# One added wait in the seven-product stage, and the first attention's transposes in three groups

## What is computed

```python
def forgetting_attention(q, k, v, logf):
    for s0 in range(0, s_len, Q_BLOCK):             # Q_BLOCK = 128
        logits = q[s0:s1] @ k[:s1].T * scale + c[s0:s1] - c[:s1]
        logits = where(kpos <= qpos, logits, -inf)
        p = softmax(logits)
        outs.append(p @ v[:s1])

def swiglu(h, w_gate_up, w_down):                   # 1024 -> 2 x 2816 -> 1024
    g, u = split(h @ w_gate_up)
    return (silu(g) * u) @ w_down
```

## Time and profile before

| | us |
|---|---|
| median of 3 timed runs | 1335.58 (1335.21 to 1336.49) |
| profiled execution, its own time | 1338.37 |
| its span, first to last instruction | 1336.6 |
| PE busy | 1313.5 (98%) |
| DVE busy | 774.5 (58%) |
| ACT busy | 614.4 (46%) |
| POOL busy | 358.3 (27%) |

### The profile page before, as it was taken

One profiled execution on the slowest core, in us unless ns is written; L12 is line 12 of the kernel. 1 busy time (PEld: TensorE's weight loads), 2 busy tenths in 40 slices (PEclk: granted clock), 3 DMA queues, 4 the chain that ended last, 5 costly groups with the idle time before them and its releaser, 6 DMA issues.

```text
span 1336.6 us, 18442 instructions
## 1 busy us (share of the span) xinstructions
PE 1313.5 (98%) x7206; PEld 1093.9 (82%) x7206; DVE 774.5 (58%) x1544; ACT 614.4 (46%) x1315; POOL 358.3 (27%) x246
## 2 busy tenths in 40 slices
PE   7999999999999999999999999999999999999999
PEld 6777887888889999998887877877878787777777
DVE  4416574333479887877234656566666666666643
ACT  4325565222435444445224446454656555556430
POOL 4013310000046556540002404142322424144210
PEclk8999999999999999999999999999999999999999
DMA  7303232332442343233235222222222222323311
GB/s 241 102 16 90 78 95 64 95 95 95 158 157 87 104 127 116 75 127 111 79 108 207 95 65 71 94 74 93 79 72 72 72 72 71 103 71 125 140 59 63
DMA packets 110103, 130.87 MB, mean 98 GB/s; under 512 B 7488, under 2 KB 87360, under 8 KB 110016
## 3 DMA queue, kind: packets, MB, share of 16 engines
q1 hardware_dynamic: 104400, 112.39, 26.3%
q10 hardware_dynamic: 5616, 17.30, 3.5%
HBM read 120.24 MB, written 9.44 MB: 97 GB/s over the span
## 4 chain that ended last, share of the span: by engine, by line
PE 81%; DVE 10%; ACT 4%; POOL 2%; issue 2%; DMA 0%; ACTq 0%; DVEq 0%
PE ps L812 13%; PE ps L814 12%; PE ps L813 12%; PE ps L817 6%; PE ps L819 6%; PE ps L818 6%; PE ps L1019 5%; PE ps L1022 5%; PE ps L1021 5%; DVE wlo L1443 3%; PE ps L1077 2%; POOL rq L1814 2%; ACT px L1394 2%; PE ps L1087 1%; ACT whi L1142 1%
## 5 line engine op out<-in xcount | busy, mean ns | idle before, releaser
L1443 DVE TENSOR_TENSOR wlo<-raw,whi 128x512 fp32r<-128x512 f32 (+1 forms) x262 | 220.0, 860 | 185.0 <-ACT whi L1142 184.3
L1142 ACT ACTIVATE whi<-raw 128x512 fp32r<-128x512 f32 (+2 forms) x338 | 210.8, 651 | 126.9 <-PE ps L814 81.8
L812 PE MATMUL ps<-whi,hth 128*128 128x512 f32 x592 | 247.7, 418 | 2.6 <-DVE wlo L1443 2.6
L814 PE MATMUL ps<-wlo,hth 128*128 128x512 f32 x592 | 233.2, 394 | 0.0
L813 PE MATMUL ps<-whi,htl 128*128 128x512 f32 x592 | 232.6, 393 | 0.0
L1844 POOL TENSOR_TENSOR wlo<-raw,whi 128x512 fp32r<-128x512 f32 (+1 forms) x76 | 91.8, 1223 | 435.4 <-ACT whi L1142 435.4
L812 PEld LDWEIGHTS ps<-whi,hth 128*128 128x128 f32 x592 | 112.1, 189 | 34.2 <-issue 9.2
L814 PEld LDWEIGHTS ps<-wlo,hth 128*128 128x128 f32 x592 | 112.0, 189 | 25.7
L813 PEld LDWEIGHTS ps<-whi,htl 128*128 128x128 f32 x592 | 112.4, 190 | 18.4
L1394 ACT ACTIVATE px<-px,nm 128x128 f32<-128x128 f32 (+3 forms) x128 | 70.7, 554 | 112.6 <-DVE nm L1758 105.0
L817 PE MATMUL ps<-hth,whi 128*128 128x512 f32 (+1 forms) x288 | 112.5, 391 | 0.0
(11 more groups left out here) (339 smaller groups left out, 2880.7 us busy)
## 6 DMA issues: line engine op xcount, KB each, us to landing
raw<-in_l_w_in SPq DMA_DIRECT2D x64, 512.0 KB, 4.7
raw<-in_w_gate_up SPq DMA_DIRECT2D x44, 512.0 KB, 4.9
raw<-in_w_in SPq DMA_DIRECT2D x14, 1024.0 KB, 5.4
raw<-in_w_down SPq DMA_DIRECT2D x10, 1024.0 KB, 5.0
raw<-in_l_w_out SPq DMA_DIRECT2D x8, 1024.0 KB, 5.2
raw<-in_w_in SPq DMA_DIRECT2D x24, 256.0 KB, 3.7
raw<-in_w_branch SPq DMA_DIRECT2D x8, 512.0 KB, 4.1
raw<-in_w_out SPq DMA_DIRECT2D x4, 1024.0 KB, 5.1
```

The source lines that it names most:

```text
L812: e.matmul(o, ah, wh[:, cs], start=a, stop=False)
L814: m = e.matmul(o, ah, wl[:, cs], start=False, stop=z)
L1142: return e.activation(out, in_, ACT.Copy, **how)
L1443: return e.tensor_tensor(out, src, hi_part.bitcast(F32), ALU.subtract)
```

## The change

The first part adds one wait to POOL's queue: the sum number 4 (T3 of block 2) starts only when `comb_d` says that U3 of block 1 is done. The second part regroups the transposes of the first attention. The ten tiles of a head go into three groups in place of four: key block 0 (4 tiles), key block 1 (3 tiles), and key blocks 2 and 3 together (3 tiles). The layout in `pth` and `ptl` stays as it was, since key block 3's columns lie right behind key block 2's. The semaphores count three a head, and `pv` waits for the third group before its key blocks 2 and 3. One bank a head fewer is dealt.

```diff
@@ attn1
             for h in (2 * j, 2 * j + 1):
-                for kb in range(TB):
-                    put("tu", h, kb, self.bank())
-                    if kb % 2:
-                        yield
+                put("tu", h, 0, self.bank())
+                put("tu", h, 1, self.bank())
+                yield
+                put("tu", h, 2, self.bank())
+                yield
                 yield
                 put("pv", h, self.bank())
@@ build
+        TILES = [[(0, qb) for qb in range(TB)], [(1, qb) for qb in range(1, TB)], [(2, 2), (2, 3), (3, 3)]]
@@ PE
                 elif kind == "tu":
-                    h, kb, b = a
+                    h, i, b = a
                     claim(b)
-                    for qb in range(kb, TB):
-                        pe.wait_ge(pn_a, AT1(h, TB - 1))
-                        m = e.transpose(ps[b][:, P * (qb - kb):P * (qb - kb) + P],
+                    pe.wait_ge(pn_a, AT1(h, TB - 1))
+                    for c, (kb, qb) in enumerate(TILES[i]):
+                        m = e.transpose(ps[b][:, P * c:P * c + P],
                                         sx[h % 2][:, QSEG[qb] + P * kb:QSEG[qb] + P * kb + P], ident[:])
                     m.then_inc(tu_pe, 1)
-                    free[b] = [(pt_lo, 4 * h + kb + 1)]
+                    free[b] = [(pt_lo, 3 * h + i + 1)]
@@ PE, pv
-                        pe.wait_ge(pt_lo, 4 * h + kb + 1)
+                        pe.wait_ge(pt_lo, 3 * h + min(kb, 2) + 1)
@@ ACT
-                    h, kb, b = a
-                    n = S - P * kb
-                    act.wait_ge(tu_pe, 4 * h + kb + 1)
+                    h, i, b = a
+                    n = P * len(TILES[i])
+                    act.wait_ge(tu_pe, 3 * h + i + 1)
...
-                    copy(pth[:, KSEG[kb]:KSEG[kb] + n], ps[b][:, 0:n]).then_inc(pt_hi, 1)
+                    copy(pth[:, KSEG[i]:KSEG[i] + n], ps[b][:, 0:n]).then_inc(pt_hi, 1)
@@ DVE
-                    dve.wait_ge(pt_hi, 4 * h + kb + 1)
+                    dve.wait_ge(pt_hi, 3 * h + i + 1)
                     lower(ptl[:, cs], ps[b][:, 0:n], pth[:, cs]).then_inc(pt_lo, 1)
@@ POOL, wt
                     else:
                         pool.wait_ge(mm, MIX_DONE)
+                    if q == 4:
+                        pool.wait_ge(comb_d, COMB(1, U3))
                     pool.wait_ge(t_p, q)
```

More of the change, by code:

```diff
@@ L1257, in _ @@
                     if j == 0:
-                        act.wait_ge(tu_pe, 4 * H1 - (4 if i == 0 else 0))
+                        act.wait_ge(tu_pe, 3 * H1 - (3 if i == 0 else 0))
                     else:
@@ L1584, in _ @@
                             if h >= 2:
-                                dve.wait_ge(tu_pe, 4 * h - 4)
+                                dve.wait_ge(tu_pe, 3 * h - 3)
                             e.tensor_tensor_reduce(
@@ L1597, in _ @@
                 elif kind == "tu":
-                    h, kb, b = a
-                    n = S - P * kb
-                    cs = slice(KSEG[kb], KSEG[kb] + n)
-                    dve.wait_ge(pt_hi, 4 * h + kb + 1)
+                    h, i, b = a
+                    n = P * len(TILES[i])
+                    cs = slice(KSEG[i], KSEG[i] + n)
+                    dve.wait_ge(pt_hi, 3 * h + i + 1)
                     lower(ptl[:, cs], ps[b][:, 0:n], pth[:, cs]).then_inc(pt_lo, 1)
```

## The result

The changed kernel takes 1340.28 us in the median (1337.32 to 1342.60), the kernel before 1335.58 us. The ratio is 1.0034, 95% interval 1.0026 to 1.0042: slower by 4.5 us by the ratio, between 3.5 and 5.6. The forecast was 1339.0.

A forecast was written before the change was run, and what follows sets the result against it. The prediction took PE, busy 98%, as the bound, so only its waits and low clock count; -3.9 + 0.4 + 3.3 + 1.6 + 0.3 + 1.6 gave +3.3 to 3.4 us on 1335.58: 1339.0, range 1333.2 to 1341.2.

The forecast's parts named there:

- What bounds the kernel, and the first wait: PE is busy 98%; its wait for C22 in block 1 (2.29 us) goes, with its clock loss: -3.9 us.
- That it comes back in block 2: Delayed POOL sums make PE wait in block 2: 0.4 us at product 3, 3.3 us for C22 at product 6.
- the wait doesn't come back: Rival: sums drain between block 2's splits before C22 is due; -2.0 us, 1333.6; chance 0.16.
- GU1 isn't blocked: Rival: block 2's products GU1 and GU0 aren't blocked by POOL's sum; -0.2 us, 1335.4; chance 0.13.
- The load at no cost: Block 3's B21/B22 load starts later, at 434.0, but lands in under 5 us, before the ninth sum asks: 0.
- the place that the walk gave it: POOL's ninth sum runs between DVE's splits T1 and T4 of block 2, ending at 443.9.
- The clock behind the C22 waits: Low clock behind block 1's wait goes (1.60 us); a fall behind block 2's wait adds 1.6 us.
- Three groups: First attention: fewer instructions gain 0, the wider last group costs +0.3 us, the bank claim +1.6 us.
- the bank: Head 7's last `pv` lands in PJ[3], so the next step, `gt`, waits for DVE's `yb_lo`: +1.6 us.
- the rival of a second fall: Rival: PE's clock also falls at 226, behind the gate unit's wait; +1.6 us, 1340.6; chance 0.20.
- The sum: Whole kernel: -3.9 + 0.4 + 3.3 + 1.6 + 0.3 + 1.6 = +3.3 to 3.4 us, forecast 1339.0.

The follow-up runs named there:

- seventh sum held: Kernel before with the wait for U3 of block 1 put on POOL's seventh sum in place of the fifth; ratio 1.0001 (0.9992 to 1.0010).
- C22 first: Kernel before with no added wait, the split of the next block's B11 put behind C22; ratio 0.9990, timed again 0.9996.
- the first four experiments: Added wait alone (1.0015) and transpose groups alone (1.0018) on the kernel before; groups with bank turn moved (0.9999); changed kernel with bank turn moved (1.0018).
- the first further profile of before: Kernel before, unchanged, one more profiled execution: C22 wait of 2.1 us in block 1, no clock fall behind it, stage 198.8 us.

## Why the prediction was right, point by point

*What bounds the kernel, and the first wait:* right. The C22 wait of block 1 goes in every profile with the added wait.

*That it comes back in block 2:* right in kind, and in size where the ninth sum was in time: 0.3 us at product 3 and 3.1 us at product 6, forecast 0.4 and 3.3. The chain behind it (the eighth sum blocks GU1, each later split finds a sum ahead) is in the rows. The rivals "the wait doesn't come back" and "GU1 isn't blocked" fall, the latter by the 2.90 us row.

*The load at no cost:* mis-sized. I wrote that such loads land in under 5 us, which is about the median of the loads of this kind (4.9 to 5.1 us in the profiles). This one lands 6.9 to 7.5 us after the seventh sum, with two loads of ACT's queue beside it that I had overlooked, so it, and not T2's split, releases the ninth sum, and in one of the four profiles with the wait on the fifth sum alone it came too late for the place that the walk gave it. There lateness was a gain: it let T4's split by and left 1.8 us in two waits. So the profiled execution of the changed kernel itself didn't go the way that was forecast; the other three had the one long wait, two of them with the clock fall.

*The clock behind the C22 waits:* mis-sized on both sides. I took 1.6 us off with certainty and put 1.6 on. It fell in three of six profiles behind the 2.1 us wait and in two of three behind the 3.1 us wait. In the sum the two terms cancelled, which hid the error, and that was luck; in the forecasts of experiments that shorten the wait and put no long one in its place it showed, as gains that were 1.2 us (seventh sum held) to 2.3 us (C22 first) too large, of which this term explains at most 1.6.

*Three groups:* right: 0.4 us for the wider group (forecast 0.3) and 1.6 for the bank; the row's 1.41 us counts from the end of the last matmul, not from when the next one was due. The clock fell behind it in none of three profiles; the rival of a second fall isn't seen. But its length alone, by which I argued, doesn't settle that: in a profile of before the clock did fall behind another wait of 1.41 us (see the last section).

*The sum:* part 1 forecast +1.4, measured +2.0 (0.8 to 3.2); part 2 forecast +1.9, measured +2.4 (1.2 to 3.6); both +3.4, measured +4.5 (3.5 to 5.6). The waits in the traces account for 2.0 us of part 2 and, from 198.8 to 200.3 us before to 199.1 to 201.6 after, for about 1 us of part 1, 2.8 at the most. So some 1.5 us of the total isn't located in a row of these stages. By the estimate from the mean granted clock the 11 executions of the changed kernel lost 9.5 us to low clock, and the 33 of the kernel before that stand beside the first four experiments lost 8.0: 1.5 us, with a standard error of 0.8. The rest of the span differs by 3.1 us, which is what the waits make. That the changed kernel really has more low clock is not shown: the added wait alone and the groups alone lost 7.9 and 7.2, no more than before. So the forecast is right by its mechanisms, the second wait and the bank, but that 1340.28 came within 1.3 us of 1339.0 rests in part on two clock terms that cancelled.

## What to carry to other kernels

A wait that holds work back in order to clear the way for something else moves that work into the next period; before adding it, walk the queues one period further and see what stands ahead of the same deadline there. A change of order (here C22 ahead of a split that isn't due for a block) takes the same work out of the way without making a backlog. It did so here in both profiles; what it gives in time is about 1 us and not settled.

When a number of buffers dealt in turn changes, look at which one the deal ends on, and who claims it next: that cost 1.6 us here, and the instructions that the change removed gave nothing that shows in the time.

A term that hangs on the clock isn't known from one profile. Read several, above all before it is put into a sum as certain.

## What the runs showed of the hardware that I had not expected

The granted clock behind one and the same wait is not the same in each execution: 2.1 us of idle PE were followed by about 3.3 us at the lower level in three profiles of six, 3.1 us in two of three, the 1.41 us near 224 in none of three, and 0.9 to 1.3 us in none of the profiles that have such waits in the stage. The length of the wait alone doesn't decide. In the second attention the first further profile of before has a wait of 1.41 us with a fall behind it; here are PE's timeline and the stretch behind. The first profile of C22 first has one of 2.66 us before 1218.50 with the clock at 1.00 behind it.

```profile
1245.66 1.30 PE L1111 MATMUL ps<-ones,osq 128*128 128x1 f32 x8 [1.41 <-DVE nm L1758]
```

```profile
1246.00:1248.00 2.00, 2.00 (x12) 2.00 (x12) 0.16 (x1) 0.00 (x0) 0.77 (x1) 0.58 0.94 360
```

DVE's splits and POOL's sums take turns when both wait: a POOL sum that waits gets in before DVE's next split, even if that is ready (landing 1.68 and 1.90 us after T2's split began). One that asks just as the next split begins comes behind it (2.27 us). So a difference of 0.4 us in when a load lands became one of 2.2 us in when C22 was done.
